# A context unit's slab asked for and split one expert block ahead in a fused two-block transformer kernel

## What is computed

```python
def expert_block(args):
    xb, e = args
    return (jax.nn.silu(xb @ w_gate[e]) * (xb @ w_up[e])) @ w_down[e]
ys = lax.map(expert_block, (xs, block_e)).reshape(n_rows, d)
out = jax.ops.segment_sum(ys * row_w[:, None], row_tok, num_segments=n_tok)
```

```python
def swiglu(x, wi, wo):
    g, u = jnp.split(x @ wi, 2, axis=-1)
    return (jax.nn.silu(g) * u) @ wo
hc = ffn_half(hc, mc, 0, norm_g[l, 0], ffn_wi[l, 0], ffn_wo[l, 0])
```

## Time and profile before

| | us |
|---|---|
| median of three executions | 3261.25 |
| the profiled execution | 3264.42 |
| its span in the trace | 3262.6 |
| expert blocks 5 to 46, in the span | about 605 to 1149 |
| TensorE busy in the whole span | 3017.6 (92%) |

### The profile page before, as it was taken

How to read it: one execution, slowest core, us unless ns; L and a number is a source line. 1 busy time by engine, 2 the same in 40 slices (tenths; PEclk the granted TensorE clock), 3 DMA queues, 4 the chain that set the end, 5 groups by cost and what they waited for, 6 DMA issues and landing times.

```text
span 3262.6 us, 52341 instructions
## 1 busy us (share of the span) xinstructions
PE 3017.6 (92%) x22245; PEld 2401.7 (74%) x22245; DVE 1493.7 (46%) x2105; ACT 990.1 (30%) x1442; POOL 365.3 (11%) x181
## 2 busy tenths in 40 slices
PE   6998967899999989999899989999899997989999
PEld 6887746577777779877566638888688886669899
DVE  6534343233323356663742234445544456571466
ACT  3212211322222244442631122222422224262343
POOL 5121100000000000122022100000000002215000
PEclk9999988899999989999999999999999998999999
DMA  6336394999999855422012222222222222204352
GB/s 239 120 139 244 131 389 168 420 406 374 377 371 384 366 205 181 154 78 78 1 40 89 78 78 91 98 95 91 78 91 101 92 92 77 91 14 181 142 181 90
DMA packets 77052, 547.58 MB, mean 168 GB/s; under 512 B 8384, under 2 KB 10432, under 8 KB 11056
## 3 DMA queue, kind: packets, MB, share of 16 engines
q1 hardware_dynamic: 76000, 540.05, 42.8%
q0 software_dynamic: 848, 4.52, 0.4%
HBM read 637.86 MB, written 1.05 MB: 196 GB/s over the span
## 4 chain that ended last, share of the span: by engine, by line
PE 82%; DVE 10%; ACT 4%; DMA 3%; issue 1%; POOL 0%; DVEq 0%; SPq 0%; POOLq 0%; ACTq 0%
PE bank L689 60%; PE bank L1017 8%; DMA ring<-slabs 3%; PE bank L1339 2%; PE bank L848 2%; PE bank L859 1%; DVE clow L2329 1%; PE bank L856 1%; ACT whi L1752 1%; ACT ht L1558 1%; PE bank L738 1%; DVE tiny L2482 1%; PE bank L1427 1%; DVE wk L2459 1%; PE bank L705 1%
## 5 line engine op out<-in xcount | busy, mean ns | idle before, releaser
L689 PE MATMUL bank<-hhi,whi 128*128 128x256 f32 (+1 forms) x1408 | 482.2, 342 | 31.2 <-DVE hlo L1975 31.2
L689 PE MATMUL bank<-hlo,whi 128*128 128x256 f32 (+1 forms) x1408 | 476.8, 339 | 0.0
L689 PE MATMUL bank<-hhi,wlo 128*128 128x256 f32 (+1 forms) x1408 | 473.2, 336 | 0.0
L1955 DVE TENSOR_TENSOR wlo<-ring,whi 128x2048 fp32r<-128x2048 f32 x132 | 298.7, 2288 | 224.1 <-ACT whi L1527 196.2
L689 PE MATMUL bank<-fhl,whi 128*128 128x256 f32 (+1 forms) x1408 | 351.6, 341 | 0.0
L689 PEld LDWEIGHTS bank<-hhi,whi 128*128 128x128 f32 x1408 | 267.2, 190 | 71.1 <-issue 29.6
L1527 ACT ACTIVATE whi<-ring 128x2048 fp32r<-128x2048 f32 x132 | 251.3, 1909 | 218.2 <-PE bank L689 211.5
L689 PEld LDWEIGHTS bank<-hhi,wlo 128*128 128x128 f32 x1408 | 268.4, 191 | 30.2
L689 PEld LDWEIGHTS bank<-hlo,whi 128*128 128x128 f32 x1408 | 268.6, 191 | 26.3
L689 PEld LDWEIGHTS bank<-fhl,whi 128*128 128x128 f32 x1408 | 240.9, 188 | 35.4 <-issue 5.3
L1017 PE MATMUL bank<-ring,wk 128*32 128x256 f32 x4064 | 248.9, 387 | 18.6 <-DMA ring<-slabs 12.5
(11 more groups left out here) (431 smaller groups left out, 5217.0 us busy)
## 6 DMA issues: line engine op xcount, KB each, us to landing
ring<-slabs SPq DMA_DIRECT2D x542, 1024.0 KB
wk<-slabs SPq DMA_DIRECT2D x45, 1024.0 KB, 11.7
ac<-slabs SPq DMA_DIRECT2D x16, 1024.0 KB, 10.7
wk<-mixp POOLq DMA_DIRECT2D x1, 1040.0 KB, 12.4
xt<-xT SPq DMA_DIRECT2D x1, 1024.0 KB, 6.4
xt<-ctxT POOLq DMA_DIRECT2D x1, 1024.0 KB, 6.1
out<-xt SPq DMA_DIRECT2D x4, 256.0 KB, 2.4
cst<-maskc POOLq DMA_DIRECT2D x1, 960.0 KB, 14.5
```

Source lines behind the costliest of these rows:

```text
L689: last = pe.matmul(o, a, b, start=k == 0, stop=k == len(pairs) - 1)
L1955: tt_(wlo_of(n), slab(n), whi_of(rel).bitcast(F32), ALU.subtract).then_inc(sem("wlo"), 1)
```

## The change

The load, ScalarE's rounding and VectorE's subtraction of a unit's slab are each moved one block earlier. SP asks for the unit slab of block b + 1 ahead of gate/up slab 2 of block b. ScalarE rounds it at the end of its block b, VectorE subtracts at the end of its block b. TensorE's order, the buffers and all waits stay.

```diff
@@ SP
                     for j in range(4):
-                        if j == 2 and b in UNIT_AT:
-                            unit_load(UNIT_AT[b])
+                        if j == 2 and b + 1 in UNIT_AT:
+                            unit_load(UNIT_AT[b + 1])
                         expert_load(b, S_MOE + gu_slab(b, j), j)
@@ ScalarE
-                if b in UNIT_AT:
-                    ctx_high(UNIT_AT[b])
                 if b < NB:
                     act.wait_ge(sem("gd"), count("gd", b + 1))
...
                 if b % GB == 1 and g + 1 < NGR:
                     owned(g + 1, 1)
+                if b + 1 in UNIT_AT:
+                    ctx_high(UNIT_AT[b + 1])
@@ VectorE
-            def ctx_unit(u):
-
-                kind, k = UNITS[u]
+            def ctx_split(u):
+
                 dve.wait_ge(sem("whi"), N_SPL + u + 1)
                 unit_wait(dve, u)
                 tt_(clow[u % 2][:, :], cslab[u % 2], cwhi(u).bitcast(F32), ALU.subtract).then_inc(sem("wlo"), 1)
+
+            def ctx_unit(u):
+
+                kind, k = UNITS[u]
...
                 if b in UNIT_AT:
                     ctx_unit(UNIT_AT[b])
+                if b + 1 in UNIT_AT:
+                    ctx_split(UNIT_AT[b + 1])
```

## The result

The changed kernel is slower: median 3315.73 us (3309.24 to 3321.64, four runs) against 3262.75 us in the same group of runs, a ratio of 1.0163 (95% interval 1.0141 to 1.0184). That is 53 us more, where 29 us more were forecast, and 1.7 us past the upper end of the range. Two later groups gave 1.0168 (1.0151 to 1.0185) and 1.0169 (1.0150 to 1.0189).

The account below looks back on a forecast made before the run. TensorE was taken to bound the kernel, transfers close behind. Split -18.5, holds +29.4, start-up +2, carry-over +12 and clock +4 made +28.9 us: 3290.2 us against the median 3261.25, range 3268 to 3314.

Parts of the forecast that it names:

- held expert block: Blocks 12, 20, 21, 25, 26, 34, 39, 44: six stall TensorE 4.0 us, 26 and 34 2.7; +29.4 us in sum.
- clock: TensorE in the eight stalls of the expert stage: lower granted clock costs 0.5 us each, +4 us (0 to 8).
- overflow blocks: Blocks 11, 16, 30, 35, 40: their own slabs 2 and 3 move nothing, so their holds cost nothing by themselves.
- start-up: Start of the expert stage, up to block 7: wanted slabs land later behind a unit slab, +2 us (1 to 4).
- The split: Expert stage: earlier rounding and subtraction remove TensorE's 18 waits for the slab's low part, -18.5 us (-18.5 to 0).
- The hold: SP's queue: expert slabs stand behind the unit load's wait for unit u - 2; unit slab then lands in 4.8 us (4.3 to 6.6).
- carry-over: Blocks 36, 37, 41, 42: slabs come up short after holds because transfers have little to spare, +12 us (5 to 14 by the walk).
- part 1: The split's walk after the unit's end at 870.21: ScalarE done at 874.95, VectorE near 875.8, TensorE wants it at 876.98.
- Rival C: Expert stage: landing takes 6.6 us and transfers bound the stage, +52 us, 3313; chance 0.09.
- A: Expert stage: the ring's stock of slabs hides the holds, only the split's gain is left, -18.5 us, 3243; chance 0.05.
- B: Expert stage: holds bite half, 2 us a stall, no carry-over or clock, about 3261; needs landings within 3 us; chance 0.08.
- D: ScalarE finds the slab unlanded or VectorE is late, so the 18.5 us of waits stay: +47 us, 3309; chance 0.06.

Follow-up runs that it names:

- expert holds alone: Changed kernel with the unit load early only in blocks 12, 20, 21, 25, 26, 34, 39 and 44, old order elsewhere: 3288.18 us, 1.0072 of the kernel before.
- overflow holds alone: Changed kernel with the unit load early only in blocks 11, 16, 30, 35 and 40, old order elsewhere: 3266.51 us, 1.0015 of the kernel before.
- unheld early loads alone: Changed kernel with the unit load early only where SP finds the buffer free or nearly so: 3246.12 us, 0.9946 of the kernel before.
- split_only: Changed kernel with SP's old load order, so only rounding and subtraction are early (the early split alone): 3240.77 us, 0.9932 of the kernel before.

## Why the prediction was right, and where it failed

The mechanism and the direction were right, and the sum was too small by 24 us. The step that failed is the price of a held expert block, 4.0 us of stall and 0.5 us of clock: the slabs land later than taken in some of these blocks, and the slow matmuls behind a stall cost about three times as much. In six of them, with expert holds alone, the two are 28.9 and 9.7 us, where 24 and 3 were forecast. Eight such blocks cost 46 to 50 us where 29.4 + 4 were forecast. The terms for the overflow blocks and for the start-up were too small as well.

- **The split: right.** -18.5 forecast, 18.6 measured in the trace of blocks 11 to 46, and TensorE has no new wait for either engine. (ScalarE now waits for some unit slabs, 22 us in 8 places of the early split alone, which holds nobody.)
- **The hold: right in mechanism and places, too small in landing.** The least landing of a unit slab is now 4.8 us (the row "DMA to landing us min/median/max: 4.8/7.3/22.9" of the trace after), the value I took. Blocks 21, 25, 34 and 44 have 4.7 to 4.9, and so has 26 in two traces of three (5.5 in the third). Blocks 20 and 39 have 5.8 to 6.2 us in all three traces, though the DMA engines were idle or nearly so when the slab was asked for. In each of these cases one instruction load (16 KB on queue q8) began 1.2 to 4.1 us behind the unit's end, while the slab was on its way. Block 12 has 6.5 to 7.3 us in the changed kernel, behind a queue still at work. Of the 38.6 us in the six blocks of the table with expert holds alone, 28.9 are the later start of slab 3, where 24 were forecast. The two others (26 and 34) were forecast at 2.7 and lost 2.2 and 3.0.
- **The clock: too small.** Put at 0.5 us a stall, from one gather in the earlier trace rows. The same row 632.53 shows a slab of 1.94 us where 0.92 to 1.07 is the rule, and I did not count it, nor a slow unit behind it. In the same six blocks it is 9.7 us, and 8.5 to 13.4 in the changed kernel, where 3 were forecast.
- **Overflow blocks "cost nothing by themselves": wrong.** I looked at when their own slabs are wanted. But the hold packs the down slabs of b - 1 and the gate/up slabs of b + 1 behind one point, the overflow block itself takes only 12.6 us (13.8 before the early split), and the burst is not through when the next block wants its slabs 2 and 3: with overflow holds alone slab 3 of block 12 is begun 8.7 us behind the end of block 11's unit, and 5.8 with none. The carry-over of 12 us was to hold this. Alone these five cost 20 us in the expert stage, and in the changed kernel 15 to 20 us stand in such blocks (17, 18, 31, 36, 37, 41, 42). Block 12's own share is on top.
- **Start-up: too small.** From the end of block 0 to that of block 10 the kernel before takes 137.1 us, the changed one 146.5, 145.2 and 146.7. That is 8 to 10 us, not 2. With the unheld early loads alone (here blocks 4, 5 and 10) it is 140.5. By difference the larger part is the holds in blocks 6 and 7; no run has these alone.
- **Two readings of the rows were off, with little effect.** In part 1 the sum from 870.64 gives 874.85, not 874.95. In the carry-over the tail was put at 3.4 us, where the earlier trace rows has 3.19; with that the slabs would have been wanted at 18.8 us instead of 19.2, and the shortfall forecast a little larger.

In sum, from the second trace of the changed kernel against the early split alone: 46 us in the eight held expert blocks (forecast 29.4 + 4), 16 in the others (forecast 12), 8 at the start (forecast 2), and -18.5 for the split, which is +52 in the trace of the expert stage. Rival C gave +52, but that the numbers meet is luck: it took a landing of 6.6 us in all eight blocks and a stage bound by transfers, where most landings are 4.8 and the DMA share fell to 0.83. Rivals A, B and D are out: holds are not hidden, landings are not under 4.3 us, the split works.

The version to keep is `split_only`: 0.7% faster than before and 2.3% faster than the change. No slab had to be asked for earlier. Before, 15 of 31 were asked for at the end of unit u - 2 already, and two buffers allow no sooner; the other 16 could be asked for up to 9 us earlier, but with the early split alone TensorE waits for none of them.

## What to carry to other kernels

Moving a load ahead in a queue moves its wait too: if the buffer comes free at the same time as before, the load gains nothing and everything that it was moved past waits with it. List what stands behind the wait, for its neighbours as well, and walk two holds in a row, since a burst that is let go late may not be through when the next one is due. And price a stall of TensorE with the slower matmuls during and behind it.

## What the runs showed of the hardware

Waits of 2.4 to 4.8 us for slab 2 were followed by the lower clock in blocks 12, 20 and 21 of the changed kernel: the granted clock was 0.77 and 0.82 in the mean around block 21's stall and 0.50 from 862 to 864, and the matmuls of the slab read between two waits took 1.93 us for 1.07. Filling the idle time with matmuls that nobody needs kept the clock at 1.00 in block 21 and took the slow matmuls of six blocks away, which had cost 8.5 to 13.4 us. That fits the Trainium skill ("TensorE: Matmul & The Clock Gate", section "Part 1: The HAM clock gate (the "warmup" mystery)"), which has the array at either 1.2 or 2.4 GHz depending on how busy it was; a shift by a factor of about 1.8 in the same instructions agrees.

A 1 MB slab asked for on an idle queue, with others right behind it, landed 4.7 to 5.0 us after its issue in most held blocks of the changed kernel. Where one instruction load of 16 KB began while it was on its way (blocks 16, 20, 35 and 39, in three traces) it landed after 5.6 to 6.3 us. In the trace after, the DMA queues show none from 852.1 to 858.7 (block 21) and this one from 831.4 to 838 (block 20):

```profile
q8 instruction: 1, 0.02, 1.3%
```

That the load is the cause is not shown by an experiment; the two went together in all twelve cases, and where the slab took 4.7 to 5.0 us no such load began between its issue and 4.2 us behind it.
